# Spreading the twelve remaining score steps of a routed-expert layer over 68 gather slots instead of 34

## The chip, the cores and the metric

One core of one Trainium2 chip runs the whole program. The metric is device time in microseconds, taken on the chip, the lower the better. Before the change three runs gave 2683.86, 2695.13 and 2700.23 us; the median is 2695.13 us.

## What is computed

The program is a two-layer backbone with 256 latent tokens and 256 context tokens of width 1024. Layer 0 mixes tokens by neighbourhood attention and bidirectional retention, layer 1 by windowed attention, and each mixer is followed by a routed-expert layer ("PEER"). Only the expert layer is shown, since the gathers around which everything is ordered come from it:

```python
def peer(h, w_q, sub_keys, u, v):
    B, T, D = h.shape
    q = (h @ w_q).reshape(B, T, PEER_HEADS, 2, PEER_QDIM // 2)
    s = jnp.einsum('bthpd,hpnd->bthpn', q, sub_keys).astype(jnp.float32)
    s1, i1 = lax.top_k(s[..., 0, :], PEER_TOPK)
    s2, i2 = lax.top_k(s[..., 1, :], PEER_TOPK)
    cand_s = (s1[..., :, None] + s2[..., None, :]).reshape(B, T, PEER_HEADS, PEER_TOPK * PEER_TOPK)
    cand_i = (i1[..., :, None] * PEER_KEYS + i2[..., None, :]).reshape(B, T, PEER_HEADS, PEER_TOPK * PEER_TOPK)
    top_s, pos = lax.top_k(cand_s, PEER_TOPK)
    idx = jnp.take_along_axis(cand_i, pos, axis=-1)
    gate = jax.nn.softmax(top_s, axis=-1)
    ...
        act = jax.nn.gelu(jnp.einsum('td,ted->te', h_i, u[i_i]), approximate=False)
        return jnp.einsum('te,ted->td', (g_i * act).astype(h.dtype), v[i_i])
```

There are 8 heads with 16 chosen experts each, so each token needs 128 rows of `u` and 128 rows of `v`, of 4 KB each. Six tiles of 128 tokens go through the expert layer: two context tiles and two latent tiles in layer 0, two latent tiles in layer 1.

## The kernel before

The program is written engine by engine (`block.sync`, `block.gpsimd`, `block.tensor`, `block.scalar`, `block.vector`). Each engine runs its own list in order and meets the others only at semaphores.

**Slots.** In the gather stretch everything is counted in slots. A slot is one of the 128 chosen experts of one tile (`S1 = 128` slots a tile, tiles 0 to 3 in the first stretch, slots 0 to 511). POOL issues for a slot one indirect DMA of `u` rows (128 partitions of 1024 float32, 512 KB) into a ring of `NU = 7` buffers, and `LAG = 36` slots later one of `v` rows, of the same size, into a ring of `NV = 7`. The loop on POOL takes two slots at a time: two `u` gathers, then two `v` gathers. A `u` gather waits until DVE has used that buffer (`u_dot`), a `v` gather until PE has (`v_used`). DVE does the dot product of a slot in one instruction, L1893. PE adds the `v` rows of two slots at every second slot, L1000, from slot 37 on. DVE also works out the indices of later slots: `route_in_parts` in five parts, at slots 11 to 15 of each 16 for the group of 16 slots that is two groups ahead, and at slots 2 to 6 for group 1.

**What runs beside the gathers.** The other work of the layer is written as generators of small steps, and a table `BESIDE` says how many steps each engine takes at which slot. `spread(costs, first, last)` lays steps out between two slots in proportion to estimated costs. PE takes a step at its slot, ACT one slot later, DVE two slots later (`ACT_AFTER, DVE_AFTER = 1, 2`); a step stands ahead of its slot's dot product on DVE and ahead of its slot's `v` matmuls on PE. Three parts of the first window's table matter here:

- `c_prep(0)[READY[0]:]`: the twelve remaining score steps (the loop index `hp` 5 to 16 in `prep`) of the two context tiles. On PE a step is eight query matmuls with `peer_w_q` (L975, which stand in the trace as 16 records) and the score matmuls of the head half before (L951); on ACT copies; on DVE the top 16 of one head half `m = hp - 1` of tile 0 (L1759 to L1769). For `m` 12 to 15 the same step does both tiles, and for `m` 4 to 11 tile 1's scores are kept and its top 16 taken later (`held_top`, slots 52 to 104, the same before and after).
- `c1`: the latent pass, that is norm1 (5 steps), projections of 14 units (30 steps), attention of 16 items (18), retention (10), output projection (13), and the first ten steps of its expert preparation. Its last twelve steps stand in a part of their own at slots 246 to 342.
- Weights come by SP in blocks of 512 KB into a ring of 5 (`wring`); a block is fetched once PE has used the block five places ahead of it. The twelve score steps use what is left of the 16 blocks of `peer_w_q`, the projections of the latent pass 28 blocks of `ab_w_in`.

With the first line of `BESIDE[0]` before the change, on PE the score steps stand at slots 1, 3, 6, 9, 12, 15, 18, 21, 24, 27, 30 and 33; norm1 begins at 34, the projections at 38, attention at 118, retention at 155, the output projection at 185 and the preparation at 213. On DVE all of it is two slots later.

Of the kernel before, what the change touches and what calls it, by code (L numbers as in the profile page):

```python
# [42 lines left out]
TOPK = 16  # L43
# [57 lines left out]
def spread(costs, first, last):  # L101

    total, at, out = sum(costs), 0.0, []
    for c in costs:
        out.append(first + int(at / total * (last - first)))
        at += c
    return out


def backbone(nc, a, out):  # L110
    with ExitStack() as ctx:
# [241 lines left out]
        def c_norm(j):  # L353
            return [2.0] + [0.5 * len(NORM[j][1])] * 4

        def c_proj(j):
            u0, u1 = U_OF[j]
            return [3.3, 3.9] * (u1 - u0) + [0.5] * 2

        def c_attn(n):  # L360
            i0, i1 = I_OF[n]
            return [2.9] * (i1 - i0) + [1.0] * 2

        def c_ret(p):
            return [4.0] * (HEADS0 + 1) + [2.0]

        def c_out(p):
            nt = len(PASS[p][1])
            return [1.8] + [0.5, 0.5, 3.3, 4.7] * nt + [3.3, 4.7] * nt

        def c_prep(p):
            nt = len(PASS[p][1])
            return [2.5] + [0.5] * (2 * nt) + [1.95 * nt] * 16 + [0.5]

        def table_of(*parts):
            out = {}
# [10 lines left out]
        WINDOWS = [(0, 4), (4, 6)]  # L387
        READY = [1 + 2 * len(tl) + 5 for _, tl in PASS]
        ROWS_TURNED = [4 * t0 + 2 * len(tl) + 2 * (e + 1) for (_, tl), t0 in zip(PASS, T_OF) for e in range(len(tl))]
        BESIDE = {0: table_of((c_prep(0)[READY[0]:], 1, 34), (c1[:-12], 34, 14 * TOPK + 8),  # L390
                              ([1.0] * 12, 2 * S1 - 10, 2 * S1 + 86), ([1.8] + [3.4] * 8 + [1.0], 2 * S1 + 86, 3 * S1 + 18),
                              (c_norm(2) + c_proj(2), 3 * S1 + 18, 3 * S1 + LAG + 4), (c2, 3 * S1 + LAG + 4, 4 * S1 + LAG - 8)),
                  4: table_of((c_prep(2)[READY[2]:], 4 * S1 + 1, 4 * S1 + 42), (c3[:-12], 4 * S1 + 42, 4 * S1 + 6 * TOPK + 8),
# [1577 lines left out]
```

How the kernel before makes its waits and increments, by code:

```python
        def w_wait(eng, key):  # L343
            n = place[key]
            eng.wait_ge(w_in[n % NW], 16 * (n // NW + 1))
            return W[:, n % NW, :].rearrange("p (k n) -> p k n", k=4 if key[0] == "wq" else 2)
# [114 lines left out]
        @block.sync  # L462
# [7 lines left out]
            sp.dma_start(sm[8:16, P:2 * P], a["c_ctx"].rearrange("(j p) -> j p", p=P)).then_inc(ld_row, 16)  # L470
            src = {"mod": lambda l: a["mod_w"][l], "in": lambda l: (a["ab_w_in"], a["swa_w_in"])[l][0],
                   "out": lambda l: (a["ab_w_out"], a["swa_w_out"])[l][0], "wq": lambda l: a["peer_w_q"][l]}
            for n, (_, kind, l, b, split, half, part, _) in enumerate(blocks):
                if n == 4:
                    sp.wait_ge(setup_t, 2)
                if n >= NW:
                    sp.wait_ge(*blocks[n - NW][7])
# [4 lines left out]
                    w = w[part * 512:(part + 1) * 512, b * BLK + half * 256:b * BLK + (half + 1) * 256]  # L482
                cols = 512 if split == "K" else 256
                sp.dma_start(W[:, n % NW, :].rearrange("p (k n) -> p k n", n=cols),
                             w.rearrange("(k p) n -> p k n", p=P)).then_inc(w_in[n % NW], 16)
            rows_out = out.rearrange("b (t p) d -> p (b t) d", p=P)
            sp.wait_ge(tile_added, len(TILE) - 1)
            sp.dma_start(rows_out[:, 0:1, :], X[:, 0:1, :]).then_inc(st_out, 16)
            sp.wait_ge(half_added, 1)
# [86 lines left out]
            def early_sums():  # L576
                pe.wait_ge(em_one, 1)
                for i in range(8):
```

## Time and profile before

| | us |
|---|---|
| the three runs | 2683.86, 2695.13, 2700.23 |
| the profiled execution, its own time | 2718.0 |
| its span, first to last instruction | 2716.2 |
| gather stretch of tiles 0 to 3, first dot product | at 336.4 |

The granted TensorE clock is 0.827 on average. The profile's page has the busy time of each engine, the span in 40 slices, the DMA queues, the chain of work that ended last, and the costliest groups of instructions. The profile's rows name the expert rows `u_rows` and `v_rows`; the instruction L1893 appears as a pair, the custom dot product and a short read of the accumulator, so that twice the number of slots stands as its count. A stretch of the span can be asked for: busy time of each engine in it, granted clock, share of time in which the 16 DMA engines are busy, and GB/s moved.

### The profile page before, as it was taken

How to read it: one execution, taken by the hardware profiler on the slowest of the kernel's cores; microseconds unless marked ns; L12 is line 12 of the kernel's file. 1: busy time of each engine (PE TensorE's matmuls, PEld its weight loads, DVE VectorE, ACT ScalarE, POOL GpSimd, SP SyncE). 2: the span in 40 equal slices, each digit the busy share in tenths (PEclk: the TensorE clock that was granted, in tenths of full speed). 3: DMA queues.
4: the chain of work that ended last, by engine and by line, in shares of the span. 5: the costliest groups of instructions: out<-in, count | busy, mean ns of one | idle time of the engine just before them, and what ended most of it. 6: DMA issues, size and time to landing. Idle time of an engine off the chain costs nothing.

```text
span 2716.2 us, 23064 instructions
## 1 busy us (share of the span) xinstructions
PE 1902.1 (70%) x7218; PEld 813.2 (30%) x7218; DVE 1733.5 (64%) x4290; ACT 384.7 (14%) x793; POOL 1709.4 (63%) x1575
## 2 busy tenths in 40 slices
PE   6999965887786885666565665678737886566556
PEld 2446652222343341222111211224532442222111
DVE  2633597675788776676655667653597966666641
ACT  1021111101222120101010111111111210101100
POOL 1100146767677777777777777773157777777775
PEclk8967987998888997888777867789868988877769
DMA  7774498999999999999999999996599999999998
GB/s 265 260 244 140 141 322 305 406 406 406 388 384 344 371 399 406 406 396 372 408 406 406 377 374 406 351 405 245 194 326 380 396 379 401 406 406 400 373 373 351
DMA packets 312521, 959.07 MB, mean 353 GB/s; under 512 B 30144, under 2 KB 65104, under 8 KB 312016
## 3 DMA queue, kind: packets, MB, share of 16 engines
q0 software_dynamic: 225792, 822.18, 78.3%
q1 hardware_dynamic: 82448, 127.47, 13.5%
q10 hardware_dynamic: 4160, 7.95, 0.8%
q8 instruction: 59, 0.97, 0.1%
q14 instruction: 62, 0.51, 0.1%
HBM read 956.43 MB, written 1.05 MB: 353 GB/s over the span
## 4 chain that ended last, share of the span: by engine, by line
POOL 30%; PE 23%; DMA 20%; DVE 14%; issue 12%; ACT 1%; SPq 0%; POOLq 0%; ACTq 0%; DVEq 0%
POOL u_rows L499 14%; POOL v_rows L499 14%; DMA v_rows<-in_peer_v,idx_turned 14%; PE ps L1000 8%; DVE u_rows L1893 5%; PE ps L669 3%; DMA u_rows<-in_peer_u,idx 3%; PE ps L914 1%; DMA wring<-in_ab_w_in 1%; PE ps L567 1%; PE ps L975 1%; PE ps L556 1%; POOL resid L499 1%; DMA u_rows<-in_peer_v,idx_turned 1%; PE ps L709 1%
## 5 line engine op out<-in xcount | busy, mean ns | idle before, releaser
L1893 DVE CUSTOM_DVE_ANT_0 u_rows<-u_rows,h 128x1024 f32<-128x1024 f32 x768 | 930.7, 1224 | 510.6 <-DMA u_rows<-in_peer_u,idx 500.6
L1000 PE MATMUL ps<-v_rows,spread_w 128*32 128x512 f32 x2636 | 838.1, 761 | 524.5 <-DMA v_rows<-in_peer_v,idx_turned 484.9
L499 POOL DMA_INDIRECT u_rows<-in_peer_u,idx x768 | 842.5, 1097 | 449.6 <-issue 220.4
L499 POOL DMA_INDIRECT v_rows<-in_peer_v,idx_turned x659 | 728.9, 1106 | 259.1 <-issue 177.1
L1000 PEld LDWEIGHTS ps<-v_rows,spread_w 128*32 128x32 f32 x2636 | 165.6, 126 | 1052.7 <-issue 1035.1
L669 PE MATMUL ps<-wring,arena 128*128 128x512 f32 x528 | 251.5, 623 | 20.7 <-DVE arena L1402 8.4
L975 PE MATMUL ps<-arena,wring 128*128 128x256 f32 (+1 forms) x1024 | 201.9, 358 | 2.7 <-ACT arena L1228 2.7
L975 PEld LDWEIGHTS ps<-arena,wring 128*128 128x128 f32 x1024 | 174.9, 216 | 54.6 <-issue 37.6
L537 POOL DMA_DIRECT2D u_rows<-in_mod_w x20 | 14.7, 735 | 217.9 <-DVE v_rows L1371 166.7
L669 PEld LDWEIGHTS ps<-wring,arena 128*128 128x128 f32 x528 | 99.6, 198 | 173.2 <-issue 140.3
L556 PE MATMUL ps<-table,arena 128*128 128x128 f32 x432 | 84.4, 324 | 75.4 <-ACT arena L1053 33.4
L556 PEld LDWEIGHTS ps<-table,arena 128*128 128x128 f32 x432 | 54.6, 161 | 152.6 <-issue 55.6
L1241 ACT ACTIVATE arena<-ps 128x256 f32<-128x256 f32 (+1 forms) x64 | 20.9, 328 | 499.2 <-PE ps L975 499.2
L1275 ACT ACTIVATE act_w<-act_w 128x16 f32<-128x16 f32 x48 | 10.4, 216 | 553.9 <-DVE act_w L1893 553.7
L951 PE MATMUL ps<-arena 128*128 128x128 f32 x192 | 38.2, 312 | 72.2 <-DVE top_idx L1769 48.8
L1000 PE MATMUL ps<-resid,spread_w 128*32 128x512 f32 x192 | 59.4, 727 | 35.8 <-DMA resid<-in_peer_v,idx_turned 34.6
L709 PE MATMUL ps<-arena 64*128 64x512 f32 (+2 forms) x128 | 76.2, 684 | 4.4 <-DVE mod_cols L1382 2.8
L567 PE MATMUL ps<-wring,silu_c 128*32 128x512 f32 x256 | 70.4, 903 | 8.1 <-DMA wring<-in_mod_w 8.1
L914 PE MATMUL ps<-wring,arena 128*128 128x512 f32 x160 | 72.4, 602 | 3.8 <-ACT arena L1210 3.8
L727 PE MATMUL ps<-arena 128*128 128x64 f32 x416 | 63.5, 299 | 3.6 <-DVE arena L1559 3.6
L1759 DVE MAX8 top_vals<-ps 128x8 f32<-128x128 f32 x88 | 23.6, 291 | 64.0 <-PE ps L951 63.4
L1000 PE MATMUL ps<-h,spread_w 128*32 128x512 f32 x96 | 63.2, 796 | 0.6 <-DMA resid<-in_peer_v,idx_turned 0.6
(232 smaller groups left out, 2008.1 us busy)
## 6 DMA issues: line engine op xcount, KB each, us to landing
wring<-in_mod_w SPq DMA_DIRECT2D x64, 512.0 KB, 5.8
wring<-in_peer_w_q SPq DMA_DIRECT2D x64, 512.0 KB, 10.4
wring<-in_ab_w_in SPq DMA_DIRECT2D x56, 512.0 KB, 8.5
u_rows<-in_peer_u,idx POOLq DMA_INDIRECT x768, 9.2
wring<-in_swa_w_in SPq DMA_DIRECT2D x24, 512.0 KB, 9.4
v_rows<-in_peer_v,idx_turned POOLq DMA_INDIRECT x659, 9.4
u_rows<-in_mod_w POOLq DMA_DIRECT2D x20, 512.0 KB, 6.2
wring<-in_ab_w_out SPq DMA_DIRECT2D x16, 512.0 KB, 6.4
```

The source lines that it names most:

```text
L499: nc.gpsimd.indirect_dma_start(out=rows, out_offset=None, in_=table, in_offset=bass.IndirectOffsetOnAxis(ap=index, axis=0)).then_inc(lande ...
L556: return nc.tensor.transpose(dst, src, ident[0:n, 0:n])
L567: mm = nc.tensor.matmul(MP(l, b)[32 * q:32 * q + 32, :], SC[:, 4 * half + q, :], w[:, q % 2, :], start=half == 0, stop=half == 1, skip_gro ...
L669: mm = nc.tensor.matmul(PS[:, (0, 1, 4)[u % 3], :], HT[:, 4 * half + k, (t % 2) * P:(t % 2 + 1) * P], w[:, k % 2, :], start=half + k == 0, ...
L709: nc.tensor.matmul(PS[:, i % 2, 0:nk], q, k, start=True, stop=True).then_inc(at_s, 1)
L727: mm = nc.tensor.matmul(PS[:, 4 + m % 2, 0:HD], PT[:, m % 2, c, :], val, start=c == 0, stop=c == len(kts) - 1)
L914: mm = nc.tensor.matmul(PS[:, u % 2, :], HT[:, 4 * half + k, (t % 2) * P:(t % 2 + 1) * P], w[:, k % 2, :], start=half + k == 0, stop=half ...
L951: mm = nc.tensor.matmul(PS[:, (4 if apart and e else 2) + m % 2, e * P:(e + 1) * P], QTB[:, m % 2, e * P:(e + 1) * P], SK[:, m, :], start= ...
L975: mm = nc.tensor.matmul(PS[:, hp % 2, 0:nt * P], w[:, k % 4, (hp % 2) * P:(hp % 2 + 1) * P], HT[:, k, lo:lo + nt * P], start=k == 0, stop= ...
L1000: mm = nc.tensor.matmul(PS[32 * q:32 * q + 32, 6 + e, :], spread_w[:, s // PAIR % 2, 32 * c:32 * c + 32], v_buffer(v_place(x)[0])[:, e * 5 ...
L1759: ins = nc.vector.max(tv[:, 0:8], s)
L1893: nc.vector.tensor_tensor_reduce(UB[:, slot % NU, :], UB[:, slot % NU, :], H2[:, g // 8 % 3, :], 1.0, 0.0, ALU.mult, ALU.add, av_[:, 0, g ...
```

## The change

One number pair in the table of the first window. The first line spreads the twelve score steps over slots 1 to `4 * TOPK + 4` = 68 in place of 34, and lays the first 86 steps of the latent pass between 68 and 232 in place of 34 and 232. Nothing is added or taken away, and the other parts keep their slots.

```diff
-        BESIDE = {0: table_of((c_prep(0)[READY[0]:], 1, 34), (c1[:-12], 34, 14 * TOPK + 8),
+        BESIDE = {0: table_of((c_prep(0)[READY[0]:], 1, 4 * TOPK + 4), (c1[:-12], 4 * TOPK + 4, 14 * TOPK + 8),
```

By the formula of `spread` the score steps then stand on PE at slots 1, 7, 13, 19, 25, 31, 37, 43, 49, 55, 61 and 67; norm1 begins at 68, the projections at 71, attention at 137, retention at 168, the output projection at 193, the preparation at 216. The other engines follow as before.

**DVE, the first gathers.** The rows below are a piece of the difference between the two orders on DVE, at the first score steps after slot 0. An L1893 pair is one slot, the five rows L1759 to L1769 are one score step of one tile, and L1793 to L1797 the first part of a routing.

```order
-L1759 MAX top_vals<-ps 128x8
-L1762 MAX_INDEX top_idx<-top_vals,ps 128x8
-L1763 MATCH_REPLACE arena<-top_vals,ps 128x128
-L1766 MAX top_vals<-arena 128x8
-L1769 MAX_INDEX top_idx<-top_vals,arena 128x8
 L1893 ISA u_rows,act_w<-u_rows,h 128x1024
 L1893 ISA act_w 128x1
```

This score step stood ahead of the dot product of slot 5 and now stands ahead of slot 9's. Of the steps that stood on DVE at slots 3 to 35 every second one leaves in this way; those at slots 3, 9, 15, 21, 27 and 33 are the ones that remain.

**PE, the first v matmuls.** Of the order on PE before the change, around the first `v` matmuls: L951 are score matmuls, L556 the sixteen transposes of norm1, L1000 the `v` matmuls, L669 the projections.

```order
L975 MATMUL ps<-arena,wring 128x256 x8
L951 MATMUL ps<-arena 128x128 x4
L556 MATMUL ps<-table,arena 128x128 x16
L1000 MATMUL ps<-v_rows,spread_w 32x512 x4
L669 MATMUL ps<-wring,arena 128x512 x4
L1000 MATMUL ps<-v_rows,spread_w 32x512 x4
```

And of the order on PE after it, from the same place:

```order
L975 MATMUL ps<-arena,wring 128x256 x8
L951 MATMUL ps<-arena 128x128 x2
L1000 MATMUL ps<-v_rows,spread_w 32x512 x12
L975 MATMUL ps<-arena,wring 128x256 x8
L951 MATMUL ps<-arena 128x128 x2
L1000 MATMUL ps<-v_rows,spread_w 32x512 x12
```

All of norm1's transposes stood ahead of the first `v` matmul; now the first `v` matmul follows a score step, three pairs of slots stand between two score steps, and norm1's transposes come after 16 pairs.

**DVE, retention.** Of the order on DVE before the change, one step of retention (L1661, L1416 to L1418 and L1668) and the first rows behind it, one slot and a part of a routing (L1804 to L1807); two more slots follow before the next retention step:

```order
L1661 TENSOR_TENSOR arena<-arena 128x512
L1416 TENSOR_SCALAR arena<-table,log_gamma 128x512
L1417 TENSOR_SCALAR arena<-table,log_gamma 128x512
L1418 TENSOR_TENSOR arena<-arena 128x512
L1668 TENSOR_TENSOR arena<-ps,arena 128x512 x2
L1893 ISA u_rows,act_w<-u_rows,h2 128x1024
L1893 ISA act_w 128x1
L1804 MAX_INDEX route_idx<-best,route_cand 128x8
L1805 TENSOR_SCALAR route_idx<-route_idx 128x16
L1806 TENSOR_SCALAR route_idx<-route_idx 128x16
L1807 CAST route_idx_f<-route_idx 128x32
```

And of the order after the change, from the end of one retention step to the end of the next:

```order
L1668 TENSOR_TENSOR arena<-ps,arena 128x512 x2
L1893 ISA u_rows,act_w<-u_rows,h2 128x1024
L1893 ISA act_w 128x1
L1893 ISA u_rows,act_w<-u_rows,h2 128x1024
L1893 ISA act_w 128x1
L1661 TENSOR_TENSOR arena<-arena 128x512
L1416 TENSOR_SCALAR arena<-table,log_gamma 128x512
L1417 TENSOR_SCALAR arena<-table,log_gamma 128x512
L1418 TENSOR_TENSOR arena<-arena 128x512
L1668 TENSOR_TENSOR arena<-ps,arena 128x512 x2
```

A retention step costs the same as before; before, the steps are laid out three to four slots apart, and after the change two to three slots apart.

## Rows read from the trace of the kernel before

**Rows 1.** The page: DMA rate in 40 slices; the gathers' queue: packets, MB, share.
```profile
GB/s 265 260 244 140 141 322 305 406 406 406 388 384 344 371 399 406 406 396 372 408 406 406 377 374 406 351 405 245 194 326 380 396 379 401 406 406 400 373 373 351
...
q0 software_dynamic: 225792, 822.18, 78.3%
```
**Rows 2.** Stretches of the span, busy us and instructions of each engine, DMA.
```profile
core 0: us, PE busy (x) PEld busy (x) DVE busy (x) ACT busy (x) POOL busy (x), PEclk, DMA share, GB/s
336.40:414.80 78.40, 48.71 (x215) 41.05 (x213) 75.70 (x251) 10.85 (x27) 37.73 (x35) 0.82 0.90 319
414.80:467.50 52.70, 32.18 (x104) 12.45 (x104) 42.91 (x116) 12.46 (x21) 34.62 (x31) 0.75 0.84 293
467.50:683.80 216.30, 171.03 (x500) 55.45 (x498) 139.88 (x337) 25.72 (x46) 156.26 (x144) 0.90 1.03 406
683.80:737.40 53.60, 41.77 (x186) 18.28 (x186) 42.46 (x105) 12.58 (x28) 37.38 (x34) 0.84 1.01 388
737.40:789.00 51.60, 42.01 (x185) 20.34 (x184) 40.86 (x105) 8.77 (x19) 39.70 (x40) 0.83 1.02 400
789.00:830.60 41.60, 34.09 (x167) 19.84 (x165) 38.60 (x79) 14.31 (x24) 30.78 (x25) 0.80 0.91 322
830.60:886.00 55.40, 33.96 (x159) 17.98 (x156) 47.39 (x97) 10.89 (x17) 43.05 (x40) 0.80 0.98 368
886.00:970.00 84.00, 68.33 (x239) 24.69 (x237) 58.92 (x120) 12.44 (x21) 62.09 (x55) 0.91 0.99 375
970.00:1020.00 50.00, 42.73 (x202) 25.51 (x200) 40.22 (x127) 12.26 (x24) 36.33 (x35) 1.00 1.03 399
1020.00:1055.00 35.00, 19.67 (x56) 3.95 (x56) 21.56 (x49) 1.90 (x4) 27.33 (x25) 0.76 1.03 409
```
**Rows 3.** The last stretch again, L1893 alone: two records a slot.
```profile
1020.00:1055.00 35.00, 16.03 (x27) 0.76 1.03 409
```
**Rows 4.** DVE in order of time: a score step of one tile, one of two.
```profile
346.64 0.30 DVE L1759 MAX8 top_vals<-ps 128x8 f32<-128x128 f32 x1
...
348.36 1.23 DVE L1893 CUSTOM_DVE_ANT_0 u_rows<-u_rows,h 128x1024 f32<-128x1024 f32 x1
...
398.17 0.49 DVE L1759 MAX8 top_vals<-ps 128x8 f32<-128x128 f32 x2
...
401.07 1.22 DVE L1893 CUSTOM_DVE_ANT_0 u_rows<-u_rows,h 128x1024 f32<-128x1024 f32 x1
```
**Rows 5.** POOL in order of time: the first v gather and the first long wait.
```profile
414.78 0.93 POOL L499 DMA_INDIRECT v_rows<-in_peer_v,idx_turned  x1 [0.30 <-issue]
...
441.85 1.78 POOL L499 DMA_INDIRECT v_rows<-in_peer_v,idx_turned  x1 [6.34 <-PE ps L1000]
```
**Rows 6.** PE in order of time, the last query matmuls, then norm1's transposes.
```profile
395.75 3.62 PE L975 MATMUL ps<-arena,wring 128*128 128x256 f32 x16
...
433.29 1.97 PE L556 MATMUL ps<-table,arena 128*128 128x128 f32 x8 [22.13 <-ACT arena L1053]
```
**Rows 7.** Two groups of PE's instructions between 441.7 and 683.8 us.
```profile
L669 PE MATMUL ps<-wring,arena 128*128 128x512 f32 x224 | 106.0, 617 | 0.0
L1000 PE MATMUL ps<-v_rows,spread_w 128*32 128x512 f32 x320 | 88.8, 695 | 45.8 <-DMA v_rows<-in_peer_v,idx_turned 45.8
```
**Rows 8.** Stretches around a later norm1 (slots 402 to 424), columns as in Rows 2.
```profile
1500.60:1520.30 19.70, 12.86 (x48) 3.85 (x45) 15.50 (x33) 5.58 (x8) 16.35 (x12) 0.83 1.03 409
1520.30:1543.50 23.20, 18.34 (x58) 6.00 (x56) 16.61 (x42) 1.67 (x2) 18.32 (x17) 1.00 0.97 354
```
**Rows 9.** DVE's waits for u rows, 683.8:737.4, 737.4:789, 830.6:886: total, times, longest.
```profile
DVE u_rows L1893 <- DMA u_rows<-in_peer_u,idx: 0.4, 1, 0.4
...
DVE u_rows L1893 <- DMA u_rows<-in_peer_u,idx: 7.6, 6, 2.7
...
DVE u_rows L1893 <- DMA u_rows<-in_peer_u,idx: 6.3, 2, 3.7
```
**Rows 10.** DVE in order of time: the first of the four instructions of a tile's addition.
```profile
817.25 0.70 DVE L1856 TENSOR_TENSOR ps<-ps,g_row 128x512 f32<-128x512 f32 x1
```

## The prediction

> **What bounds the kernel now.** I read the page first. The DMA rate stands at 406 GB/s in slice after slice, and the gathers alone are 822 MB [rows 1]. At 406 GB/s those bytes need 2025 us. The kernel is therefore bound by DMA wherever the rate is 406, and the time that can be won or lost by moving steps is the time in which the DMA engines are not at that rate. Call idle of a stretch its length minus its bytes at 406 GB/s. Then I read the stretches in which the rate is lower [rows 2]:
>
> - 336.4 to 414.8 us, the first gathers, `u` only: 319 GB/s, so 78.4 x (1 - 319/406) = 16.8 us idle. DVE is busy 75.7 of 78.4 us: it is the bound.
> - 414.8 (the first `v` gather [rows 5]) to 467.5 us: 293 GB/s, 14.7 us idle. DVE is busy only 42.9 of 52.7. POOL waits once for 6.34 us for PE to free a `v` buffer [rows 5], and PE had been idle 22.13 us before norm1's transposes, which stand ahead of its first `v` matmul [rows 6].
> - 467.5 to 683.8, the projections: 406, no idle.
> - 683.8 to 789, attention: 2.4 + 0.8 = 3.2 us idle. 789 to 886, retention: 41.6 x (1 - 322/406) = 8.6 and 5.2, together 13.8 us; in its first half DVE is busy 38.6 of 41.6 us.
> - 886 to 970, output projection, 6.4 us; 970 to 1020, 0.9 us.
>
> A transfer of 512 KB costs 524,288 B / 406 GB/s = 1.29 us of DMA, so a slot with `u` and `v` costs 2.58 us. A slot costs DVE (dot product, routing, weighing), where nothing else runs beside, 21.56 us for 27 records, or 13.5 slots: 1.60 us [rows 2, 3].
>
> **Gain before the first v gather.** The first `v` gather stands on POOL behind the `u` gather that waits for the dot product of slot 30. Ahead of that dot product DVE had ten moved steps (slots 3, 5, 8, 11, 14, 17, 20, 23, 26, 29), eight of one tile and two of both; now it has five of one tile (3, 9, 15, 21, 27). A step of one tile takes 348.36 - 346.64 = 1.72 us, of both 401.07 - 398.17 = 2.90 us [rows 4]. So 3 x 1.72 + 2 x 2.90 = 11.0 us of the bounding engine go from this stretch. They are not all won, since bytes leave it too. By the first `v` gather PE had finished all query matmuls, the last sixteen records at 395.75 + 3.62 us [rows 6]; now those of four of the sixteen head halves (steps at 43, 49, 55, 61) stand behind the first `v` matmuls, so four blocks of weights of 1.29 us, 5.2 us in all, are fetched later, where the DMA has no idle time to hide them. Gain 11.0 - 5.2 = 5.8 us.
>
> The Trainium skill speaks of this in "DMA: Bandwidth & Descriptors", section "Issuing engines are not separate DMA queues": transfers started by different engines run on the same 16 DMA engines and interleave. By that rule the weight blocks on SP's queue and the gathers on POOL's pay from one purse; if queues were separate the gain here would be 11.0. This trace agrees: in the projections, where both run, the sum stays at 406 GB/s.
>
> **Gain after the first v gather.** Here norm1 no longer stands ahead of the first `v` matmul; the score steps that now stand at 37 to 67 need PE for 3.62 us of query matmuls each [rows 6] in six slots, and DVE at most 2.9 us in six slots, 1.60 + 0.48 and, for each of the eight kept top 16s in slots 52 to 104, one more step of some 1.7 us, before as after, against 2.58 us of DMA a slot. So the stretch should be at 406 GB/s almost at once. I leave 2 us for the start (it cannot be under 0) and win 14.7 - 2 = 12.7 us. The bounds are 14.7, and 8.4 if what is lost is only POOL's one wait of 6.34 and some 2 us of refilling.
>
> **Cost of norm1 at slots 68 to 71.** It now runs in saturated DMA. The nearest row is the later norm1 of two tiles: 409 GB/s, nothing lost, then 354 GB/s in the 23.2 us behind it, 3.0 us [rows 8]. PE's wait there is covered by the seven `v` buffers. I take 1 us, of 0 to 3.
>
> **Cost of closing up the latent pass.** 198 slots become 164, and each stage keeps its work while its slots bring fewer bytes. A slot that is taken from a stage costs nothing where DMA is the bound, and 2.58 - 1.60 = 0.98 us where DVE is.
> - Projections, 80 to 66 slots. DVE has room. In 242.1 us PE spent 106.0 on projections and 88.8 on `v` matmuls, and waited 45.8 for `v` rows [rows 7]. In 66 slots it needs 106 + 88.8 x 66/80 + 5 of transposes = 184 us; DMA needs 66 x 2.58 + 28 x 1.29 = 206 us. PE comes to 89% and stays under; I take 2 us, of 0 to 6.
> - Attention 37 to 31 slots, retention 30 to 25. If every slot removed were DVE's: 11 x 0.98 = 10.8 us. By halves, the time in which DVE doesn't wait for `u` rows (the stretch less its waits for them [rows 2, 9]) against the DMA's need (the stretch's bytes at 406 GB/s), each less 1.60 or 2.58 a slot: first half of attention 53.2 - 4.8 = 48.4 against 51.2 - 7.7 = 43.5; second 44.0 - 4.8 + 2.8 (four instructions of 0.70 [rows 10], the tile's addition at slot 164, which was in retention and is now in attention) = 42.0 against 43.1; first half of retention 41.6 - 2.8 - 3.2 = 35.6 against 33.0 - 5.2 = 27.8; second 49.1 - 4.8 = 44.3 against 50.2 - 7.7 = 42.5. Idle 4.9 + 0 + 7.8 + 1.8 = 14.5. The same count of the kernel before gives 2.0 + 0 + 8.6 + 0 = 10.6 where 17.0 was lost, so 6.4 us come from unevenness inside the halves, and I keep them: 20.9 against 17.0. I take 4 us, between 2 and 10.8.
> - Output projection, 28 to 23 slots: PE is busy 68.3 of 84 us. Less 5 x 1.1 it needs 63 against 64 us of DMA. If PE were the bound the five slots would cost 5 x (2.58 - 1.1) = 7.4; I take 3, of 0 to 7.4.
> - Preparation, 16 to 13 slots, at 399 GB/s and DVE busy 40.2 of 50: 1 us, of 0 to 3.
>
> **Sum.** Gain 5.8 + 12.7 = 18.5; cost 1 + 2 + 4 + 3 + 1 = 11. Net -7.5 us. All of it lies ahead of slot 232 and nothing behind has slack, since at slots 232 to 400 the rate is mostly 406 again: the net goes into the time whole. The profiled time of 2718.0 us becomes 2710.5, and the median, 23 us lower, 2695.1 - 7.5 = 2688 us.
>
> **Rivals.**
> 1. The latent pass becomes the bound and gives all of it back. Every cost at its upper end: 3 + 6 + 10.8 + 7.4 + 3 = 30 us against a gain of 18.5 or less, so +12 us or more, 2707 us, and with the low gain of 14.2 +16, 2711. It speaks for it that retention is already short of DVE (38.6 of 41.6 busy) and PE near 89% in the projections; against it that attention's second half has 7.6 us of DVE's waits for `u` rows left [rows 9]. It decides when the latent pass loses more than 18.5 us more than now, that is when the idle of 683.8 to 1020 rises from 24 to over 40 us.
> 2. The latent pass has more room than I count. Costs at the lower end, 2 us, gain 20: -18 us, 2677 us. It would need retention, whose first half has 8.6 us more of DVE than of DMA already, to be covered by the two rings of seven buffers.
> 3. The change does nothing to speak of: DMA bytes decide, what DVE gives up early comes back as weight blocks, and the stall of norm1 only moves from slot 36 to slot 70. Then the gain is 5.8 + 12.7 less the 6.3 us of POOL's wait, and the cost 11: -1, 2694 us. For it: bytes are the same. Against it: at slot 70 DVE and POOL have full rings, at slot 36 no `v` row had been used yet.
>
> **How the numbers follow.** A measurement of this kernel can hardly tell less than 1%, 27 us, from no change; its three runs lie 16 us apart. Chances: the forecast (-2 to -14 us) 0.45; rival 3 (within 2 us of nothing or so) 0.18; rival 1 (+3 and more) 0.22; rival 2 (-15 and more) 0.15. Of rival 1 perhaps a quarter goes past +27, of rival 2 a quarter past -27 with the scatter of a median. So faster 0.04, same 0.90, slower 0.06. The range takes -18 and +16 and adds 3 us of scatter: 2674 to 2714 us; the forecast's own is 2681 to 2693.
>
> **What would show it.** Right: the first `v` gather some 67 us behind the first dot product instead of 78; no PE idle time of 22 us ahead of it; 400 GB/s and over from there to attention; retention's stretch at a lower rate than 322 to 368, with DVE busy over 93%; equal bytes. Wrong: POOL waiting for PE (`ps` L1000) by over 10 us in the projections, which says PE was the bound there; the stretch behind the first `v` gather still under 350 GB/s; or POOL's waits at norm1 of more than 5 us.

## The result

The changed kernel took 2720.68 us (median of 20 runs, 2705.06 to 2738.24), the kernel before 2700.19 us (20 runs, 2679.48 to 2722.75). The ratio of the two is 1.0067, 95% interval 1.0043 to 1.0090: about 18 us slower, where 7.5 us faster was forecast and 2674 to 2714 was the range.

The two profiled spans, 2716.2 us before and 2718.5 us after, hardly differ, for two reasons: in the changed kernel's execution the gathers began at 330.1 us instead of 336.4, and what follows slot 504 took 6.4 us less. The start is no part of the change: between the profiled executions of this study it lies anywhere from 308.8 to 338.1 us. Counted from the first dot product to that of slot 504, the changed kernel took 1483.5 us and the kernel before 1468.4: 15.1 us more. All that is located below lies in this stretch.

The first view is the one of [rows 2]: stretches of the changed kernel's span, busy us and instructions of each engine, granted clock, DMA share, GB/s. Its bounds are those at which slots 0, 31, 49, 64 and 80 are reached, then the end of the projections, attention, retention and output projection on DVE.

```profile
core 0: us, PE busy (x) PEld busy (x) DVE busy (x) ACT busy (x) POOL busy (x), PEclk, DMA share, GB/s
330.10:397.70 67.60, 31.17 (x127) 25.56 (x125) 65.59 (x195) 7.49 (x18) 38.50 (x35) 0.76 0.93 328
397.70:440.10 42.40, 22.48 (x74) 8.89 (x75) 33.11 (x88) 5.95 (x16) 33.84 (x29) 0.74 0.96 349
440.10:485.40 45.30, 31.33 (x123) 15.37 (x122) 35.26 (x120) 4.33 (x8) 35.65 (x32) 0.88 1.01 392
485.40:546.80 61.40, 38.64 (x119) 13.81 (x120) 40.47 (x110) 9.16 (x16) 37.93 (x34) 0.78 0.82 305
546.80:730.40 183.60, 153.89 (x456) 51.49 (x454) 113.44 (x258) 25.72 (x44) 135.07 (x119) 0.94 1.03 405
730.40:829.50 99.10, 80.37 (x336) 36.50 (x334) 77.53 (x192) 20.08 (x46) 61.33 (x60) 0.83 0.95 364
829.50:914.50 85.00, 59.69 (x303) 34.88 (x302) 78.62 (x164) 23.61 (x38) 61.31 (x54) 0.82 0.93 337
914.50:987.60 73.10, 62.05 (x221) 24.68 (x219) 46.02 (x88) 8.52 (x14) 50.82 (x45) 0.90 0.92 346
```

One row has no partner before the change. At 485.4 to 546.8 us, slots 64 to 80, the DMA moved 305 GB/s, and no engine was near its limit: PE 38.6, DVE 40.5, POOL 37.9 of 61.4 us busy. In the kernel before the same slots lie inside a stretch at 406 GB/s [rows 2, third row].

The chain behind that row shows on PE, in order of time (start, us, engine and line, what it works on, and in brackets the idle time ahead of it and what ended it).

```profile
496.63 1.91 PE L1000 MATMUL ps<-v_rows,spread_w 128*32 128x512 f32 x8 [0.74 <-DMA v_rows<-in_peer_v,idx_turned]
510.05 1.97 PE L556 MATMUL ps<-table,arena 128*128 128x128 f32 x8 [11.51 <-ACT arena L1053]
511.95 3.63 PE L1000 MATMUL ps<-v_rows,spread_w 128*32 128x512 f32 x8
515.51 1.22 PE L556 MATMUL ps<-table,arena 128*128 128x128 f32 x8
521.14 6.13 PE L669 MATMUL ps<-wring,arena 128*128 128x512 f32 x8 [4.41 <-DVE arena L1402]
527.19 1.94 PE L1000 MATMUL ps<-v_rows,spread_w 128*32 128x512 f32 x16
```

And on POOL, at the gathers of `v` rows:

```profile
515.86 0.94 POOL L499 DMA_INDIRECT v_rows<-in_peer_v,idx_turned  x1 [4.83 <-PE ps L1000]
...
529.39 0.94 POOL L499 DMA_INDIRECT v_rows<-in_peer_v,idx_turned  x1 [8.87 <-PE ps L1000]
```

PE stood 11.51 us before norm1's transposes and 4.41 us more before the first projection. The `v` matmuls are queued behind both, so from 498.54 us, where PE stopped, to 527.19 only one pair of `v` rows was used (at 511.95). POOL then ran out of `v` buffers, waited 4.83 and 8.87 us, and with it waited the `u` gathers of the same loop.

DVE's rows between 500 and 507 us say what the first of the two stops was waiting for:

```profile
500.65 0.50 DVE L1759 MAX8 top_vals<-ps 128x8 f32<-128x128 f32 x2
...
503.55 1.22 DVE L1893 CUSTOM_DVE_ANT_0 u_rows<-u_rows,h 128x1024 f32<-128x1024 f32 x1
504.70 1.22 DVE L1323 CUSTOM_DVE_ANT_0 arena<-resid 128x1024 f32<-128x1024 f32 x1
505.85 1.22 DVE L1323 CUSTOM_DVE_ANT_0 arena<-resid 128x1024 f32<-128x1024 f32 x1
```

The last score step (slot 69 on DVE), one dot product, and norm1's statistics (slot 70) followed on one another. PE's transposes stand at slot 69 of its own list and need both: the statistics, through ACT's scaled copies (L1053), and the last score step, since norm1's first wait on PE is for all sixteen score steps of the tile pair (their PSUM banks are used again). The second stop, of 4.41 us, ended with DVE's last eviction of norm1 (L1402), which DVE took at 520.09 us, behind one of the kept top 16s (slot 72).

For all kernels below, one table. Each number is the DMA idle time of a range of slots in one profiled execution, worked out as in the prediction: the time from the end of one dot product to the end of another, less the bytes of the packets that started in it at 406 GB/s. A range 31-49 holds the slots 31 to 48.

| kernel | 0-31 | 31-49 | 49-64 | 64-80 | 80-120 | 120-157 | 157-195 | 195-232 | 232-256 | sum |
|---|---|---|---|---|---|---|---|---|---|---|
| before | 16.3 | 15.2 | 0.1 | -0.1 | 0.2 | 3.2 | 17.2 | 3.8 | 0.0 | 55.8 |
| e0_before_again | 17.0 | 15.8 | 0.0 | -0.1 | 0.2 | 5.8 | 19.5 | 4.0 | 1.7 | 63.8 |
| after | 13.0 | 6.0 | 1.6 | 15.3 | 0.3 | 0.4 | 24.3 | 11.6 | 1.4 | 73.9 |
| g2_after_again | 14.4 | 8.4 | 1.3 | 15.3 | 0.3 | 0.4 | 28.1 | 14.2 | 6.6 | 89.0 |
| e1_pass_only | 17.3 | 9.0 | 3.8 | 13.4 | 0.3 | 0.4 | 24.0 | 14.1 | 4.3 | 86.5 |
| e2_scores_by_56 | 14.5 | 5.3 | 2.9 | 10.4 | 0.4 | 0.8 | 27.3 | 13.9 | 6.8 | 82.4 |
| e3_norm1_stats_early | 14.9 | 5.3 | 3.6 | 5.1 | 0.3 | 1.4 | 17.2 | 11.6 | 5.9 | 65.2 |
| f1_stats_ahead_of_before | 16.5 | 14.5 | -0.1 | 0.0 | 0.5 | 6.6 | 18.4 | 4.1 | 2.9 | 63.2 |
| f2_stats_ahead_of_after | 13.4 | 6.1 | 2.9 | 7.6 | 0.4 | 3.9 | 18.1 | 13.8 | 5.9 | 72.1 |
| f3_late_stages_as_before | 13.4 | 6.1 | 1.8 | 9.2 | 5.5 | 3.6 | 25.3 | 4.5 | 3.9 | 73.2 |
| f4_scores_by_44 | 14.2 | 4.7 | 6.3 | 0.2 | 0.2 | 5.0 | 21.0 | 4.1 | 2.5 | 58.1 |
| g3_gap_after | 14.0 | 6.5 | 3.9 | 5.4 | 0.4 | 0.6 | 24.1 | 7.8 | 5.2 | 68.0 |
| g4_gap_before | 16.6 | 11.1 | 1.4 | 0.0 | 0.3 | 5.1 | 14.8 | 4.1 | 5.2 | 58.6 |
| g1_scores_by_50 | 13.9 | 6.7 | 2.4 | 1.1 | 0.6 | 6.0 | 25.0 | 3.6 | 2.9 | 62.2 |

Kernels whose names begin with e, f and g ran on three different chips, each group beside the kernel before on its own chip; on them the kernel before took 2802.39, 2814.58 and 2799.05 us, 4% more than on the chip of the main comparison. Times are therefore compared as ratios to the kernel before. A ratio counts the runs within 1.5% of the fastest of its kernel, which leaves out three of ten for e3, three of twelve for g2 and g4, and at most two for the others, among them the profiled executions of e3, f4 and g1.

### The profile page after: what moved, and what is told of

Read it like the earlier page. It is cut to its first block, busy times and chain, and to the rows that moved or that the text cites. A ratio compares the mean times of both kernels' runs of the same rounds, so it can differ in the third digit from the quotient of the medians.

```text
span 2718.5 us, 23065 instructions
## 1 busy us (share of the span) xinstructions
PE 1891.1 (70%) x7218; PEld 804.9 (30%) x7218; DVE 1732.6 (64%) x4290; ACT 381.1 (14%) x791; POOL 1718.4 (63%) x1575
## 3 DMA queue, kind: packets, MB, share of 16 engines
q1 hardware_dynamic: 82448, 127.47, 13.4%
## 4 chain that ended last, share of the span: by engine, by line
POOL 27%; PE 24%; DMA 22%; DVE 13%; issue 12%; ACT 1%; SPq 0%; ACTq 0%; POOLq 0%; DVEq 0%
DMA v_rows<-in_peer_v,idx_turned 14%; POOL u_rows L499 13%; POOL v_rows L499 12%; PE ps L1000 9%; DVE u_rows L1893 5%; DMA u_rows<-in_peer_u,idx 4%; PE ps L669 3%; DMA wring<-in_ab_w_in 2%; PE ps L975 2%; PE ps L556 1%; PE ps L914 1%; PE ps L567 1%; PE ps L709 1%; POOL resid L499 1%; PE ps L727 1%
## 5 line engine op out<-in xcount | busy, mean ns | idle before, releaser
L1893 DVE CUSTOM_DVE_ANT_0 u_rows<-u_rows,h 128x1024 f32<-128x1024 f32 x768 | 930.5, 1224 | 510.9 <-DMA u_rows<-in_peer_u,idx 501.0
L1000 PE MATMUL ps<-v_rows,spread_w 128*32 128x512 f32 x2636 | 840.5, 758 | 524.1 <-DMA v_rows<-in_peer_v,idx_turned 484.1
L499 POOL DMA_INDIRECT u_rows<-in_peer_u,idx x768 | 855.5, 1114 | 431.0 <-issue 222.1
L1000 PEld LDWEIGHTS ps<-v_rows,spread_w 128*32 128x32 f32 x2636 | 164.7, 125 | 1054.1 <-issue 1038.0
L669 PE MATMUL ps<-wring,arena 128*128 128x512 f32 x528 | 254.6, 627 | 27.1 <-DVE arena L1402 13.1
L669 PEld LDWEIGHTS ps<-wring,arena 128*128 128x128 f32 x528 | 99.7, 199 | 180.5 <-issue 138.9
L556 PE MATMUL ps<-table,arena 128*128 128x128 f32 x432 | 83.0, 321 | 66.3 <-ACT arena L1125 24.2
L951 PE MATMUL ps<-arena 128*128 128x128 f32 x192 | 37.1, 306 | 86.3 <-DVE top_idx L1769 39.8
L556 PEld LDWEIGHTS ps<-table,arena 128*128 128x128 f32 x432 | 54.3, 159 | 143.3 <-issue 54.6
L1275 ACT ACTIVATE act_w<-act_w 128x16 f32<-128x16 f32 x48 | 10.4, 216 | 531.0 <-DVE act_w L1893 530.8
L1000 PE MATMUL ps<-resid,spread_w 128*32 128x512 f32 x192 | 56.9, 699 | 31.2 <-DMA resid<-in_peer_v,idx_turned 30.6
L709 PE MATMUL ps<-arena 64*128 64x512 f32 (+2 forms) x128 | 73.9, 664 | 5.1 <-DVE mod_cols L1382 2.8
L1759 DVE MAX8 top_vals<-ps 128x8 f32<-128x128 f32 x88 | 23.7, 292 | 66.6 <-PE ps L951 65.9
L1000 PE MATMUL ps<-h,spread_w 128*32 128x512 f32 x96 | 63.4, 798 | 0.7 <-DMA resid<-in_peer_v,idx_turned 0.7
```

What stands on the lines that cost most here:

```text
L499: nc.gpsimd.indirect_dma_start(out=rows, out_offset=None, in_=table, in_offset=bass.IndirectOffsetOnAxis(ap=index, axis=0)).then_inc(lande ...
L556: return nc.tensor.transpose(dst, src, ident[0:n, 0:n])
L669: mm = nc.tensor.matmul(PS[:, (0, 1, 4)[u % 3], :], HT[:, 4 * half + k, (t % 2) * P:(t % 2 + 1) * P], w[:, k % 2, :], start=half + k == 0, ...
L709: nc.tensor.matmul(PS[:, i % 2, 0:nk], q, k, start=True, stop=True).then_inc(at_s, 1)
L951: mm = nc.tensor.matmul(PS[:, (4 if apart and e else 2) + m % 2, e * P:(e + 1) * P], QTB[:, m % 2, e * P:(e + 1) * P], SK[:, m, :], start= ...
L1000: mm = nc.tensor.matmul(PS[32 * q:32 * q + 32, 6 + e, :], spread_w[:, s // PAIR % 2, 32 * c:32 * c + 32], v_buffer(v_place(x)[0])[:, e * 5 ...
```

## The experiments

### Only the latent pass moved, and what stands ahead of norm1

Three kernels and a control, on one chip. The edits are to the first line of `BESIDE[0]` of the changed kernel. In `e1_pass_only` the score steps keep their old slots:

```diff
-(c_prep(0)[READY[0]:], 1, 4 * TOPK + 4), (c1[:-12], 4 * TOPK + 4, 14 * TOPK + 8),
+(c_prep(0)[READY[0]:], 1, 34), (c1[:-12], 4 * TOPK + 4, 14 * TOPK + 8),
```

In `e2_scores_by_56` they end twelve slots ahead of norm1:

```diff
-(c_prep(0)[READY[0]:], 1, 4 * TOPK + 4), (c1[:-12], 4 * TOPK + 4, 14 * TOPK + 8),
+(c_prep(0)[READY[0]:], 1, 56), (c1[:-12], 4 * TOPK + 4, 14 * TOPK + 8),
```

And in `e3_norm1_stats_early` norm1's first step, the statistics, stands at slot 60 besides:

```diff
-(c_prep(0)[READY[0]:], 1, 4 * TOPK + 4), (c1[:-12], 4 * TOPK + 4, 14 * TOPK + 8),
+(c_prep(0)[READY[0]:], 1, 56), (c1[:1], 60, 61), (c1[1:-12], 4 * TOPK + 4, 14 * TOPK + 8),
```

> Only half of the change: the score steps stay at slots 1 to 34 and the latent pass alone moves to slots 68 to 232, so slots 34 to 68 hold nothing but dot products. Theory P (pile-up): the 15.3 us of DMA idle time that the changed kernel has at slots 64 to 80 come from DVE having the kept top 16 of slot 68, the last score step of both tiles at 69 and norm1's statistics at 70 behind one another while PE waits for norm1. Here the score step is gone from there, so slots 64 to 80 should lose 5 us or less. Theory R (ring): norm1 and the first projections cost this wherever they meet saturated DMA, since PE's list holds the v matmuls behind them. Then slots 64 to 80 lose 12 to 16 us here too. Both expect slots 120 to 232 to lose some 35 us as in the changed kernel (27 before), and slots 31 to 49 under 6 us (15 before). Whole time against the kernel before: P +2 to +8 us, R +14 to +20 us.

Measured: ratio 1.0107 (1.0060 to 1.0154), by the ratio about 30 us more than the kernel before, past the range of either theory, and no better than the whole change (the intervals overlap). Slots 64 to 80 lost 13.4 us. Theory P in its strong form falls: with the score steps gone since slot 34, moving the latent pass to slot 68 still costs most of the loss. Slots 31 to 49 lost 9.0 us instead of 15.8 (the "under 6" of both theories was wrong), and slots 120 to 232 lost 38.5. The rows of waits on PE in slots 64 to 80, total us, times and longest:

```profile
PE ps L1000 <- DMA v_rows<-in_peer_v,idx_turned: 8.6, 2, 5.7
PE ps L556 <- ACT arena L1053: 6.9, 1, 6.9
PE ps L669 <- DVE arena L1402: 4.4, 1, 4.4
```

Without a score step in front the wait for the statistics is 6.9 us, not 11.5. The second stop is unchanged, 4.4 us.

> As the changed kernel, but the score steps are spread over slots 1 to 56 (the last at 55), the latent pass from 68 to 232 as in the change. P: slots 64 to 80 lose 5 us or less, the whole is 8 to 12 us faster than the changed kernel, about +4 to +8 us against the kernel before. R: slots 64 to 80 lose 12 to 16 us, the whole within 4 us of the changed kernel.

Measured: 1.0030 (0.9986 to 1.0074), and 10.4 us lost at slots 64 to 80; the wait for the statistics was 7.5 us:

```profile
PE ps L556 <- ACT arena L1053: 7.5, 1, 7.5
```

That is between the two theories, and in the range of neither: 4.9 of 15.3 us gone with the score step, 10.4 left. The second stop was 4.4 us again.

> As e2_scores_by_56, and the first step of norm1 (DVE's statistics, ACT's scaled copies; PE has nothing in it) at slot 60 in place of 68, so that PE finds its input ready at slot 69. P: nothing more than e2_scores_by_56 (within 3 us of it at slots 64 to 80). R in the form that the wait for the statistics is the cause (PE idle 11.5 us there in the changed kernel): slots 64 to 80 lose under 5 us here and over 10 in e2_scores_by_56. R in the form that it is the chain of transposes, evictions and first projections behind it: still over 8 us here.

Measured: 1.0022 (0.9977 to 1.0068), and 5.1 us at slots 64 to 80. PE's waits in those slots:

```profile
PE ps L1000 <- DMA v_rows<-in_peer_v,idx_turned: 7.0, 2, 4.2
PE ps L669 <- issue: 1.3, 1, 1.3
PE ps L556 <- DVE arena L1402: 1.2, 2, 1.0
```

The loss is half of e2's. But two things changed between e2 and e3: the wait for ACT is gone, and the stop ahead of the first projection fell from 4.4 to 1.3 us, since the edit also moves later steps by up to two slots (norm1's last transposes stand at slot 69 on PE, in e2 at 71). So the 5.3 us are not the statistics' alone. Retention (157 to 195) lost 17.2 us here against 27.3; that difference is not explained by PE's wait and is taken up below.

> The kernel before once more, as a control: how far the DMA idle time of each range of slots repeats from one profiled execution to another, and how far two equal kernels differ in the comparison. Expected: each range within 2 us of the kernel before, the sum over slots 0 to 504 within 4 us of 82.6, the ratio within 0.3% of 1.

Measured: 0.9990 (0.9955 to 1.0025). Up to slot 120 the ranges repeat within 0.7 us; behind it within 2.6 us each, which sum to 6.8 more. Up to slot 504 it is 120.6 us against 82.6, outside the 4 us expected: the slots behind 256 lost 30 us more on that chip. The changed kernel and its repeat g2 are further apart in places: 1.4 and 2.4 us in the first two ranges, 0.1 or less at slots 64 to 80. So ranges ahead of slot 49 can be compared to some 2 us, those from there to slot 120 to about 1, later ones only to several, and those behind slot 256 not across chips.

### The two waits apart

`f1` and `f2` take norm1's first step out of the gather stretch, on DVE, ACT and PE alike, and put it ahead of slot 0; the step's cost leaves `c1`:

```diff
-        c1 = c_norm(1) + c_proj(1) + c_attn(1) + c_ret(1) + c_out(1) + c_prep(1)
+        c1 = c_norm(1)[1:] + c_proj(1) + c_attn(1) + c_ret(1) + c_out(1) + c_prep(1)
...
             rest = ready_and_route(0)
-            gathers(0, 4, chain(rest, norm1(1), proj(1), attn(1), ret(1), outp(1), prep(1),
+            n1 = norm1(1)
+            next(n1)
+            gathers(0, 4, chain(rest, n1, proj(1), attn(1), ret(1), outp(1), prep(1),
```

> The kernel before with the first step of norm1 (DVE's statistics and ACT's scaled copies of the latent tiles) taken out of the gather stretch and put ahead of it, where DVE waits 5.7 us for the first rows; the score steps stay at slots 1 to 34, the remaining steps of the pass at 34 to 232. Theory R (PE's wait for norm1's input, with the v matmuls queued behind it, empties the DMA queues): slots 31 to 49 lose 6 to 10 us of DMA time instead of 15 to 16, the whole -6 to -10 us. Rival S (the loss at slots 31 to 49 is that of DVE's score steps and of starting the v stream, norm1 has no part): still 13 us or more there, the whole within 3 us.

Measured: 1.0018 (0.9987 to 1.0048); 14.5 us at slots 31 to 49. As expected by rival S, and my theory as I had put it fell. But the trace says that it was not S's reason either. PE in f1, at norm1's transposes:

```profile
403.18 1.94 PE L556 MATMUL ps<-table,arena 128*128 128x128 f32 x8 [15.76 <-issue]
```

and DVE at the same time:

```profile
402.75 0.28 DVE L1773 FIND_INDEX8 top_idx<-top_vals,arena 128x8 uint32<-128x128 f32 x1
403.07 1.22 DVE L1897 CUSTOM_DVE_ANT_0 u_rows<-u_rows,h 128x1024 f32<-128x1024 f32 x1
```

PE still stood 15.76 us before norm1's transposes, and started at the moment at which DVE ended the last score step (L1773, which is L1769 four lines further down). With the statistics ready PE waits for the other of the two.

> The changed kernel with the same edit: norm1's first step ahead of the gathers, score steps at 1 to 68, the rest of the pass at 68 to 232. R: PE waits under 2 us for norm1's input (11.5 us in the changed kernel), slots 64 to 80 lose 3 to 7 us instead of 15.3, the whole is some 10 us faster than the changed kernel, +3 to +8 us against the kernel before. S: slots 64 to 80 still lose over 10 us (a double score step and a kept top 16 on DVE right ahead of the transposes), the whole +12 to +18 us.

Measured: 1.0051 (1.0014 to 1.0089); 7.6 us at slots 64 to 80. Here too a wait remained, on PE and, at its end, on DVE:

```profile
504.46 1.94 PE L556 MATMUL ps<-table,arena 128*128 128x128 f32 x8 [9.92 <-remote]
```

```profile
504.35 1.23 DVE L1897 CUSTOM_DVE_ANT_0 u_rows<-u_rows,h 128x1024 f32<-128x1024 f32 x1 [3.57 <-remote]
```

DVE's last instruction of the last score step ended at 500.78 us. The 3.6 us behind it, in which both engines stood, have no releaser in the trace, and their cause is open.

Four kernels with the latent pass at slot 68 look like a square: neither wait taken away (after) 15.3 us; the score step taken away (e2) 10.4; the statistics taken away (f2) 7.6; both (e3) 5.1. It is not a clean one. In f2 and e3 norm1's later steps stand up to two slots earlier, and the second stop, 4.4 us in the changed kernel and e2, is 1.3 us in e3 and absent in f2. What that stop is worth the next kernel shows.

> The changed kernel with only norm1 and the projections closed up (slots 68 to 118), and attention, retention, output projection and preparation at their slots of the kernel before (118 to 232). Theory D (closing up attention, retention and the output projection costs what it is over the kernel before at slots 120 to 256, 13.6 us): that range loses 24 to 31 us as in the kernel before and its control, instead of 38 to 43; slots 64 to 80 lose 13 to 18 us as in the changed kernel; the projections in 47 slots make PE the bound (106 + 52 + 5 = 163 us of PE against 47 x 2.58 + 36 = 157 us of DMA), so slots 80 to 120 lose 5 to 15 us instead of 0.3. Rival: the loss at 120 to 256 stays at 38 or more, so it doesn't come from the closing up.

The edit: `(c1[:35], 4 * TOPK + 4, 118), (c1[35:-12], 118, 14 * TOPK + 8)` in place of `(c1[:-12], 4 * TOPK + 4, 14 * TOPK + 8)`. Measured: 1.0027 (0.9994 to 1.0059). The output projection's range, slots 195 to 232, went back to 4.5 us, from 11.6 and 14.2 in the two executions of the changed kernel. Retention's range did not: 25.3 us, so for that part the rival holds. Slots 120 to 256 together lost 37.3 us, where theory D expected 24 to 31 and the rival 38 or more. The projections lost 5.5 us with PE close to its bound, as expected.

Slots 64 to 80 lost 9.2 us instead of the 13 to 18 expected, and PE's rows say why:

```profile
498.71 1.97 PE L556 MATMUL ps<-table,arena 128*128 128x128 f32 x8 [11.49 <-ACT arena L1053]
...
506.64 3.70 PE L669 MATMUL ps<-wring,arena 128*128 128x512 f32 x8 [1.09 <-DVE arena L1402]
```

The first stop is whole. The second is 1.09 us instead of 4.41: in this table norm1's last transposes stand one slot earlier, and DVE evicts them ahead of the kept top 16 of slot 72 instead of behind it. POOL's longest wait for PE in these slots fell from 8.9 to 3.7 us. Nothing else differs in these slots but the spacing of the projections, so some 6 of the 15.3 us hang on the second stop, though it is the shorter one. Stops of 11.5 and 1.1 us (f3) cost 9.2 us, stops of 6.9 and 4.4 (e1) 13.4. How the rest divides between the statistics and the last score step these kernels do not separate.

> A try at a faster kernel: norm1's first step ahead of the gathers, score steps over slots 1 to 44, the rest of norm1 and the projections over 46 to 118, everything from attention on at the slots of the kernel before. By R and D: slots 0 to 31 lose 14 to 15 us (16.3 in the kernel before), 31 to 64 together 8 to 12 (15.3), 64 to 120 under 2, 120 to 256 as before; the whole -5 to -12 us against the kernel before, and within 4 us of f1_stats_ahead_of_before.

Measured: 0.9974 (0.9934 to 1.0015), which does not tell it from the kernel before; the traces give 58.1 us of idle time up to slot 256, against 55.8 and 63.8 in the two executions of the kernel before. Up to slot 120 the ranges are as expected: 14.2, 11.0 at slots 31 to 64, and 0.4. The table's line is `(c_prep(0)[READY[0]:], 1, 44), (c1[:34], 46, 118), (c1[34:-12], 118, 14 * TOPK + 8)` with the `n1` edit above.

### A gap of four slots

If PE's list meets DVE's too early, it should be enough to leave a few slots between the step that DVE does and the step that PE needs it for.
`g3_gap_after` does that in the changed kernel:

```diff
-(c_prep(0)[READY[0]:], 1, 4 * TOPK + 4), (c1[:-12], 4 * TOPK + 4, 14 * TOPK + 8),
+(c_prep(0)[READY[0]:], 1, 4 * TOPK + 4), (c1[:1], 4 * TOPK + 4, 70), (c1[1:-12], 72, 14 * TOPK + 8),
```

and `g4_gap_before` in the kernel before, with the late stages at their old slots:

```diff
-(c_prep(0)[READY[0]:], 1, 34), (c1[:-12], 34, 14 * TOPK + 8),
+(c_prep(0)[READY[0]:], 1, 34), (c1[:1], 34, 35), (c1[1:35], 40, 118), (c1[35:-12], 118, 14 * TOPK + 8),
```

> The changed kernel with norm1's first step left at slot 68 and the rest of the pass started at 72 in place of 68, to end at 232 as before. By the order on PE, its transposes stood at slot 69 and waited for two steps of DVE that stand at 69 and 70, the last score step and norm1's statistics; here both lie behind when PE gets to slot 72. Theory W (those two waits, each with the v matmuls queued behind it, are the loss): PE waits under 3 us for norm1's input (11.5 in the changed kernel), slots 64 to 80 lose 3 to 7 us instead of 15.3, and the whole is 6 to 12 us faster than the changed kernel. Rival C (the loss is PE catching up when projections begin in saturated DMA): still 10 us or more there, the whole within 3 us of the changed kernel.

Measured: 0.9989 (0.9954 to 1.0024) to the kernel before, where the changed kernel on the same chip had 1.0070 (1.0029 to 1.0112). Slots 64 to 80 lost 5.4 us instead of 15.3. The row of slots 64 to 80, with the columns of the first view, of g3:

```profile
470.30:524.30 54.00, 35.94 (x109) 12.00 (x106) 37.96 (x104) 8.47 (x14) 39.39 (x36) 0.78 0.97 365
```

and of the changed kernel again (g2) on the same chip:

```profile
474.30:531.00 56.70, 38.90 (x119) 14.03 (x120) 40.20 (x110) 9.17 (x16) 35.38 (x31) 0.77 0.82 296
```

365 GB/s instead of 296. PE's waits for norm1's input in g3 came to 4.4 and 3.1 us (the first is still the statistics; "under 3" was too little), and POOL's longest wait for PE was 3.2 us, where it was 8.9 in the changed kernel:

```profile
PE ps L556 <- ACT arena L1053: 4.4, 1, 4.4
...
PE ps L556 <- DVE arena L1402: 3.1, 1, 3.1
```

The sum up to slot 256 fell by 21 us against the changed kernel on this chip, of which 9.9 at slots 64 to 80 and 6.4 at 195 to 232, which I had not expected to change.

> The changed kernel once more, as a control on this chip: slots 64 to 80 lose 13 to 17 us, slots 80 to 256 38 to 44 us, slots 0 to 49 18 to 21 us; the ratio to the kernel before 1.005 to 1.009.

Measured: 1.0070 (1.0029 to 1.0112), the ratio of the main comparison again, and 15.3 us at slots 64 to 80 to the tenth. Slots 0 to 49 lost 22.8 us and slots 80 to 256 49.6, both more than expected (18 to 21, 38 to 44).

> The kernel before with the same kind of gap: score steps at 1 to 34, norm1's first step at 34, its rest and the projections from 40 to 118 in place of 35 to 118, everything from attention on as before. Now the first v matmul (slot 37) stands ahead of norm1's transposes on PE. W: slots 31 to 64 lose 6 to 11 us instead of 15.3 to 15.8, the whole is -5 to -9 us against the kernel before. Rival C: 13 us or more are still lost there, the whole within 3 us.

Measured: 0.9952 (0.9917 to 0.9987), about 13 us less than the kernel before on that chip. The medians of all twelve runs and of all 35 of the kernel before are 2794.06 and 2799.05 us, only 5 us apart, so that it is faster is likely and not shown. Slots 31 to 49 lost 11.1 us instead of 15.8, and 31 to 64 together 12.5: less gained there than W expects. The sum up to slot 256 is 5.2 us lower than in the control, so more than half of the 13 us is not located.

> A try at a faster kernel: norm1's first step ahead of the gathers, score steps over slots 1 to 50, the rest of norm1 and the projections over 56 to 118, attention and all behind it at the slots of the kernel before. W: slots 0 to 80 lose 22 to 26 us (31.6 and 32.7 in the kernel before), slots 80 to 256 as before, the whole -6 to -10 us against the kernel before. C: slots 49 to 80 lose 10 us or more and the whole is no faster than the kernel before.

The line `(c_prep(0)[READY[0]:], 1, 50), (c1[:34], 56, 118), (c1[34:-12], 118, 14 * TOPK + 8)` with the `n1` edit. Measured: 0.9956 (0.9917 to 0.9995). Slots 0 to 80 lost 24.1 us, within what W expects, against 32.7 in the control: 8.6 us is what spreading the score steps is worth there when norm1 does not stop PE and the late stages keep their slots. Slots 80 to 256 did not stay as before: from slot 120 on they lost 37.4 us, against 24.1 and 30.9 in the two executions of the kernel before. The sum up to slot 256 is thus only 1.6 us lower than in the control, while the time is some 12 us shorter, and the traces do not say where these lie.

## Why the prediction was wrong

Step by step, on the chip of the main comparison:

- **DVE's time ahead of the first `v` gather**: right. The first `v` gather came 67.6 us after the first dot product, as the row shows (330.1 to 397.72), where 67 was forecast.

```profile
397.72 0.94 POOL L499 DMA_INDIRECT v_rows<-in_peer_v,idx_turned  x1 [0.30 <-issue]
```

- **Gains of 5.8 and 12.7 us**: 3.3 (slots 0 to 31) and 9.2 (31 to 49), less 1.5 lost at 49 to 64. Right in kind, 11.0 in place of 18.5 us. Two terms are mis-sized. From slots 0 to 31 went 10.8 us, where 11.0 was forecast, but 3.0 MB of bytes went with them, 7.5 us and not 5.2. And the "2 us for the start": 6.0 us of idle time stayed at slots 31 to 49, though POOL waited for nothing but 0.3 us there. In e1, where the score steps are all done by then and norm1 is away, 9.0 us stayed.
- **Cost of norm1 at slots 68 to 71**: this is the step that failed. It was put at 1 us, of 0 to 3, with "PE's wait there is covered by the seven `v` buffers". It cost 15.4 us. The precedent, the later norm1 of [rows 8], was the wrong row: in its table no score step and no kept top 16 stands in the slots ahead of it, and PE waited 1.85 us there, not 11.5. The same trace held a less mild one. At the norm1 behind it PE stood 5.87 us before the first projection, and the DMA ran at 320 GB/s (columns as in the first view):

```profile
1588.85 6.43 PE L669 MATMUL ps<-wring,arena 128*128 128x512 f32 x8 [5.87 <-DVE arena L1402]
...
1575.00:1600.00 25.00, 15.81 (x59) 5.59 (x52) 20.15 (x50) 2.65 (x3) 18.79 (x16) 0.75 0.92 320
```

  What the order shows and I did not price: PE takes its step two slots before DVE, norm1's transposes need DVE's statistics and DVE's last score step, both now stand on DVE at slots 69 and 70, and all `v` matmuls of those slots are queued behind the transposes; then the projections stop PE once more, for DVE's evictions. As an estimate, the seven buffers cover a stop of some 9 us (the ring holds 7 slots of 2.58 us, and a gather of `v` rows lands 9.4 us after its issue in the median of the kernel before, 8.5 in the changed one), and PE's stops came to 16 us in 23. With four slots of distance (g3) the loss fell from 15.3 to 5.4 us on one chip, and the ratio from 1.0070 to 0.9989.
- **The stall only moves from slot 36 to 70**: that was rival 3's mechanism, and I had argued against it that the rings are full at slot 70. They were; a full ring is what let POOL go on for two more pairs, and then it stopped for 4.83 and 8.87 us.
- **Projections, 2 us**: 0.1. PE was busy 153.9 of 183.6 us and the DMA stayed at 405 GB/s. The bound held: when f3 gave them 47 slots instead of 66, PE was busy 122.5 of 130.1 us at slots 80 to 120, and 5.5 us were lost.
- **Attention and retention, +4 us**: 24.7 in place of 20.4 us (slots 120 to 195), +4.3. Right on this chip, but not shown to come from closing up: with retention at its old slots the range lost 14.8 to 25.3 us in seven executions, with it closed up 17.2 to 28.1; attention and retention together lost 19.9 to 31.0 us with the old slots and 18.6 to 28.5 closed up.
- **Output projection, +3 us of 0 to 7.4**: 7.8 us more, at the edge. Here closing up is the cause: seven executions with the old slots lost 3.6 to 4.5 us at slots 195 to 232, seven with the closed-up ones 7.8 to 14.2. The trace shows the same kind of stop as at norm1. PE stands before the rows of the output projection until DVE has done the last retention step and the group normalisation:

```profile
913.36 3.75 PE L611 MATMUL ps<-table,mod_cols 128*128 128x128 f32 x16 [14.95 <-issue]
```

  DVE's last instruction of it (L1696) ended at 913.26 us, and POOL waited 8.13 us for PE, until 919.99. In the kernel before PE stood 9.0 us there, and POOL's longest wait was 4.2 us.
- **Sum**: forecast +18.5 - 11 = 7.5 us gained; measured in the traces up to slot 504, 11.0 gained, 15.4 lost at norm1, 4.3 and 7.8 behind it, and 1.4 gained in all the rest: 15.1 lost. Rival 1 had the right sign and size, by another way: it spread the loss over all stages, and more than half of what was lost stood at norm1. Its own condition, over 40 us of idle time from attention to preparation, was not met: slots 120 to 232 lost 36.3 us, 24.1 before.
- **The signs**: two of the three for "wrong" came, 349 GB/s behind the first `v` gather (under 350) and a wait of 8.87 us on POOL at norm1 (over 5). The third came too and says nothing: POOL waited 16.7 us for PE in the projections, but 21.4 us in the kernel before, both at 405 to 406 GB/s.

The prediction weighed the rule of the Trainium skill ("DMA: Bandwidth & Descriptors", "Issuing engines are not separate DMA queues") that transfers started by different engines share the 16 DMA engines. The trace agrees: in the projections gathers and weight blocks together again moved 405 GB/s, and in slots 0 to 31 only 3.3 of the 10.8 us were won, since the bytes that left were paid for later. Up to slot 256 both kernels moved the same 282 MB.

**What stays open.** How the first stop divides between the statistics and the last score step. What costs the 5 us that e3 and g3 still lose at slots 64 to 80, e3 with stops of 2.5 us in all. Why retention's range loses 15 us in one execution (g4) and 25 in another (f3, g1) with the same table from slot 118 on. Why g3 lost less at the output projection. Where the shorter times of g4 and g1 come from. Each kernel has one profiled execution, apart from the kernel before and the changed one, which have two.

## What to carry to other kernels

When steps are moved in a hand-made order, look at each place where an engine's list waits for a step that another engine takes later in its own list, and ask what is queued behind that wait: a full ring covers the stop only as long as the ring lasts, and here two stops close together, 11.5 and 4.4 us, cost more than everything that the move gained. A short stop right behind a long one is dear: with it reduced to 1.1 us the loss was 9.2 us instead of 15.3. Leaving four slots between the step and the one that needs it took 10 of those 15 us away. A precedent for a wait is worth as much as what stands ahead of it in the list is alike.

## What the hardware showed that I had not expected

A burst of gathers can stay below the plateau although POOL waits for no other engine. In the changed kernel between 397.7 and 440.1 us it issued gathers back to back; its waits there were these:

```profile
POOL v_rows L499 <- issue: 4.3, 14, 0.3
POOL u_rows L499 <- issue: 4.3, 14, 0.3
POOL v_rows L499 <- PE ps L1000: 0.3, 1, 0.3
```

With 33.8 us busy they fill the stretch. The mean was 349 GB/s, not 406. An issue took 0.94 us at the least, with 0.30 us ahead of it, which would be enough for 512 KB at 423 GB/s, but many took longer, as these two:

```profile
403.55 1.88 POOL L499 DMA_INDIRECT v_rows<-in_peer_v,idx_turned  x1 [0.31 <-issue]
405.73 1.99 POOL L499 DMA_INDIRECT v_rows<-in_peer_v,idx_turned  x1 [0.30 <-issue]
```

What makes an issue take 1.9 us I did not test, so whether POOL or the DMA behind it set this rate is open.

Chips differ by more than the change: 2700 us on one and 2799 to 2815 us on three others for the same kernel, and on the three others all profiled executions lost 48 to 61 us of DMA time at slots 256 to 504, where the two on the first chip lost 26.8 and 23.7. Ahead of slot 120 the kernel before lost the same on two chips, to 0.7 us in each range.
